# Attention pairs on one core: order of projections and pairs, banks of the turns, and the engine of some biases

## What is computed

```python
proj = h @ w_in[l]
qa, ka, va, qb, ckv, qi, ki, wi = jnp.split(proj, offsets, axis=-1)
out_a = dilated_mixture(qa, ka, va, slopes_a)      # A heads
q_lat = jnp.einsum('bthd,hdr->bthr', qb, w_uk[l])
o_lat = sparse_attention(qi, ki, wi * IDX_SCALE, q_lat, ckv, slopes_b)   # B heads
out_b = jnp.einsum('bthr,hrd->bthd', o_lat, w_uv[l])
x = x + ga1 * (jnp.concatenate([out_a, out_b]) @ w_out[l])
```

## Time and profile before

| | us |
|---|---|
| median of 3 runs | 2023.68 (2023.48 to 2025.96) |
| profiled execution | 2021.82, span 2020.0 |
| busy: PE, DVE, ACT, POOL | 1947.8, 1048.7, 447.2, 1183.6 |
| stretch of the eight pairs, 1515.80 to 1597.35 | 81.55, PE busy in 60.14 of it |

### The profile page before, as it was taken

The page is one execution under the profiler, slowest core; times in us unless marked ns, Lnnn a source line. Parts: engine busy times, 40 slices in busy tenths (PEclk is TensorE's granted clock), DMA queues, the critical chain, the costliest instruction groups (busy, mean ns, idle before and its releaser), DMA issues.

```text
span 2020.0 us, 25249 instructions
## 1 busy us (share of the span) xinstructions
PE 1947.8 (96%) x8772; PEld 1563.7 (77%) x8772; DVE 1048.7 (52%) x1588; ACT 447.2 (22%) x762; POOL 1183.6 (59%) x907
## 2 busy tenths in 40 slices
PE   7999999999999999998999999999997899999998
PEld 6787868888888877655888888886775588888886
DVE  5566257766646353557666663234857563232222
ACT  3302342112110022432221111012116421111100
POOL 3653325878877956223688787743550157666673
PEclk7999999999999999998999999999999999999999
DMA  7432223555555422111355553321210023232232
GB/s 298 167 125 73 94 94 104 188 187 203 188 200 179 156 91 83 42 42 46 133 201 193 194 188 127 104 95 63 84 63 22 11 84 104 93 101 97 95 113 73
DMA packets 67518, 242.25 MB, mean 120 GB/s; under 512 B 7642, under 2 KB 8026, under 8 KB 67458
## 3 DMA queue, kind: packets, MB, share of 16 engines
q1 hardware_dynamic: 65536, 237.01, 34.2%
q10 hardware_dynamic: 1922, 4.40, 0.6%
HBM read 239.28 MB, written 2.10 MB: 119 GB/s over the span
## 4 chain that ended last, share of the span: by engine, by line
PE 89%; DVE 4%; ACT 3%; issue 2%; DMA 1%; POOL 1%; SPq 0%; DVEq 0%; ACTq 0%; POOLq 0%
PE gemm L443 24%; PE gemm L445 23%; PE gemm L444 23%; PE gemm L470 2%; PE gemm L472 2%; PE gemm L471 2%; DMA w_raw<-wstream 1%; PE mix L646 1%; PE mix L443 1%; PE gemm L799 1%; PE mix L444 1%; PE mix L445 1%; PE mix L952 1%; PE gemm L813 1%; PE mix L554 1%
## 5 line engine op out<-in xcount | busy, mean ns | idle before, releaser
L427 POOL TENSOR_TENSOR w_lo<-w_raw,w_hi 128x1024 fp32r<-128x1024 f32 x302 | 741.1, 2454 | 25.2
L443 PE MATMUL gemm<-h_hi,w_hi 128*128 128x512 f32 x1616 | 635.4, 393 | 14.3 <-DVE h_lo L1123 6.4
L444 PE MATMUL gemm<-h_lo,w_hi 128*128 128x512 f32 x1616 | 631.1, 391 | 0.0
L445 PE MATMUL gemm<-h_hi,w_lo 128*128 128x512 f32 x1616 | 631.0, 390 | 0.0
L424 POOL TENSOR_TENSOR pool_gate<-pool_gate 128x1 f32<-128x1 f32 x298 | 104.2, 350 | 764.6 <-PE gemm L445 619.7
L443 PEld LDWEIGHTS gemm<-h_hi,w_hi 128*128 128x128 f32 x1616 | 305.0, 189 | 83.9 <-issue 13.4
L425 POOL TENSOR_SCALAR w_hi<-w_raw 128x1024 fp32r<-128x1024 f32 x302 | 351.1, 1163 | 18.4 <-DMA w_raw<-wstream 18.4
L445 PEld LDWEIGHTS gemm<-h_hi,w_lo 128*128 128x128 f32 x1616 | 304.7, 189 | 64.0
L444 PEld LDWEIGHTS gemm<-h_lo,w_hi 128*128 128x128 f32 x1616 | 305.2, 189 | 62.7
L1017 DVE CUSTOM_DVE_ANT_0 ada_raw<-ada_raw,c_act 128x1024 f32<-128x1024 f32 x128 | 219.4, 1730 | 106.2 <-DMA ada_raw<-adastream 106.2
L445 PE MATMUL gemm<-p_hi,w_lo 128*128 128x512 f32 x528 | 205.4, 389 | 0.0
(11 more groups left out here) (323 smaller groups left out, 1999.9 us busy)
## 6 DMA issues: line engine op xcount, KB each, us to landing
w_raw<-wstream SPq DMA_DIRECT2D x302, 512.0 KB, 3.5
ada_raw<-adastream SPq DMA_DIRECT2D x128, 512.0 KB, 4.3
a_early<-adastream SPq DMA_DIRECT2D x8, 1024.0 KB, 13.2
out<-x_res SPq DMA_DIRECT2D x8, 256.0 KB, 2.2
x_res<-x_in SPq DMA_DIRECT2D x2, 512.0 KB, 6.4
c_act<-c_in ACTq DMA_DIRECT2D x2, 512.0 KB, 7.2
x_res<-x_in ACTq DMA_DIRECT2D x2, 512.0 KB, 9.0
b_dist<-const_in ACTq DMA_DIRECT2D x1, 512.0 KB
```

The source lines that it names most:

```text
L427: pool.tensor_tensor(wlo[s][:], raw[:, u % RAW, :], whi[s][:].bitcast(F32), ALU.subtract).then_inc(w_split, 1)
L443: pe.matmul(out_ap, w_h, r_h, start=first, stop=False)
L444: pe.matmul(out_ap, w_h, r_l, start=False, stop=False)
L445: return pe.matmul(out_ap, w_l, r_h, start=False, stop=last)
```

## The change

The value chunks come first in `attn_in`, and their banks are evicted to `VA` right behind them. The A heads' query and key tiles alternate, so that the first four hold pairs 0 and 1. scores(0) start behind the latent values; then come the four tiles of pairs 2 and 3, scores(1), the first B query chunk, and the pairs. The other three B query chunks are cut into eighths and stand between the turns of pairs 0, 1 and 2 (`query_part`), in gemm bank 1; so the turns of pairs 0 to 3 use gemm bank 0 alone, each waiting for the copy of the one before. Since the high parts of the hidden state are still in use, ScalarE keeps the results of pairs 0 and 1 in T2 and makes their high parts at pair 2; VectorE makes the three low parts at p = 3. Biases of odd heads from head 5 on are made by GpSimd, in two instructions for an A head and five for a B head, between its splits of chunks (`bias` in its block); before each it waits for the logits four heads back. VectorE makes the even ones.

```diff
@@ -63,7 +63,7 @@
           ("ffn1", 44, (11, 11, 11, 11)), ("down1", 24, (2, 2, 2, 2)), ("idx_in", 6, (2, 2, 1, 1)),
-          ("attn_in", 16, (5, 5, 3, 3)), ("attn_out", 8, (2, 2, 2, 2)), ("ffn2", 44, (11, 11, 11, 11)),
+          ("attn_in", 16, (4, 7, 3, 2)), ("attn_out", 8, (2, 2, 2, 2)), ("ffn2", 44, (11, 11, 11, 11)),
@@ -430,11 +430,52 @@
                 split_at(u, 0, u, u >= SPL)
-            with pool.Fori(1, NCHUNK // 4) as b:
+            def one(n):
+                split_at(n, n // 4, n % 4, True)
+            steps = [0]
+            def bias(g):
+                if g == 5:
+                    pool.wait_ge(small_loaded, 112)
+                if g == 9:
+                    pool.wait_ge(sig("mask_rows"), 1)
+                pool.wait_ge(sig("att_z"), g - 3)
+                steps[0] += 1
+                if g < 8:
+                    pool.tensor_scalar(BI[:, g % 4, 0:T], DL[:, 0:T], -SLOPE_A[g], 0.0, ALU.mult, ALU.add).then_inc(sig("bias_slope"), 1)
+                    pool.wait_ge(sig("bias_slope"), steps[0])
+                    pool.tensor_tensor(BI[:, g % 4, 0:T], BI[:, g % 4, 0:T], DL[:, T:2 * T], ALU.add).then_inc(sig("att_b_odd"), 1)
+                else:
+                    pool.tensor_scalar(T2[:, 12, :], DL[:, 0:T], -SLOPE_B[g - 8], 0.0, ALU.mult, ALU.add).then_inc(sig("bias_slope"), 1)
+                    pool.wait_ge(sig("bias_slope"), steps[0])
+                    for j in range(NTB):
+                        seg = slice(OFF_J[j], OFF_J[j] + P * (j + 1))
+                        ins = pool.tensor_tensor(BI[:, g % 4, seg], T2[:, 12, 384 - P * j:T], SC[:, seg], ALU.add)
+                    ins.then_inc(sig("att_b_odd"), 1)
+                    pool.wait_ge(sig("att_b_odd"), steps[0])
+            ahead = N0["attn_out"] + 1
+            with pool.Fori(1, ahead // 4) as b:
                     split_at(4 * b + u, b, u, True)
-            for u in range(NCHUNK % 4):
-                split_at(NCHUNK // 4 * 4 + u, NCHUNK // 4, u, True)
+            for n in range(ahead // 4 * 4, ahead):
+                one(n)
+            for p in range(3):
+                bias(2 * p + 5)
+                one(ahead + p)
+            for g in range(11, 16, 2):
+                bias(g)
+            after = (ahead + 3 + 3) // 4
+            for n in range(ahead + 3, 4 * after):
+                one(n)
+            with pool.Fori(after, NCHUNK // 4) as b:
+                for u in range(4):
+                    split_at(4 * b + u, b, u, True)
+            for n in range(NCHUNK // 4 * 4, NCHUNK):
+                one(n)
@@ -917,15 +958,16 @@
             mm.then_inc(norm_sum, 1)
-            def attn_tiles(first):
-                for u in range(4):
-                    tile_chunk(N0["attn_in"] + first + u, (N0["attn_in"] + u) % SPL, u, G0["attn_in"][u] + first // 4)
-            attn_tiles(0)
+            def attn_tile(c, bank, use):
+                n = N0["attn_in"] + c
+                tile_chunk(n, n % SPL, bank, G0["attn_in"][bank] + use)
+            token_body(N0["attn_in"], N0["attn_in"], list(G0["attn_in"]))
             bcast(rstdps, bc[0])
-            attn_tiles(4)
+            for u in range(4):
+                attn_tile(4 + u, u, 1)
@@ -933,15 +975,14 @@
                 pe.matmul(M[j][:], T2[:, 5, j * P:(j + 1) * P], wuv[:], start=True, stop=True).then_inc(sig("vb_mm"), 1)
-            token_body(N0["attn_in"] + 8, N0["attn_in"] + 8, [g + 2 for g in G0["attn_in"]])
                 else:
-                    if p == 4:
-                        pe.wait_ge(gfree[1], G0["attn_out"][1])
+                    if p >= 4:
+                        pe.wait_ge(gfree[1], G0["attn_in"][1] + 3 + p - 3)
@@ -956,25 +997,45 @@
-            def turn(p, pieces):
-                for c in pieces:
-                    n = 5 * p + c
-                    pe.wait_ge(sig("att_p"), 2 * p + (1 if c < 2 else 2))
-                    if n < 2:
-                        pe.wait_ge(gfree[n], G0["attn_out"][n])
-                    else:
-                        pe.wait_ge(sig("att_c"), n - 1)
-                    for a, i, o in PIECES[c]:
-                        z = Z[(2 * p + a) % 4]
-                        for j in range(i, NTB):
-                            mm = pe.transpose(G[n % 2][:, o + P * (j - i):o + P * (j - i) + P],
-                                              z[:, OFF_J[j] + i * P:OFF_J[j] + (i + 1) * P], const("ident"))
-                    mm.then_inc(sig("att_t"), 1)
+            def turn_bank(n):
+                return G[0] if n < 20 else G[n % 2]
+            def turn(p, c):
+                n = 5 * p + c
+                pe.wait_ge(sig("att_p"), 2 * p + (1 if c < 2 else 2))
+                if n == 0:
+                    pe.wait_ge(gfree[0], G0["attn_out"][0])
+                elif n <= 20:
+                    pe.wait_ge(sig("att_c"), n)
+                else:
+                    pe.wait_ge(sig("att_c"), n - 1)
+                for a, i, o in PIECES[c]:
+                    z = Z[(2 * p + a) % 4]
+                    for j in range(i, NTB):
+                        mm = pe.transpose(turn_bank(n)[:, o + P * (j - i):o + P * (j - i) + P],
+                                          z[:, OFF_J[j] + i * P:OFF_J[j] + (i + 1) * P], const("ident"))
+                mm.then_inc(sig("att_t"), 1)
+            def query_part(u, first, count):
+                n = N0["attn_in"] + 12 + u
+                s = n % SPL
+                if first == 0:
+                    pe.wait_ge(w_split, n + 1)
+                    pe.wait_ge(gfree[1], G0["attn_in"][1] + 3 + u)
+                for k in range(first, first + count):
+                    mm = three(G[1][:], whi[s][:, k * P:(k + 1) * P], wlo[s][:, k * P:(k + 1) * P],
+                               Hhi[:, k, :], Hlo[:, k, :], k == 0, k == KT - 1)
+                if first + count == KT:
+                    mm.then_inc(pe_done, 1)
                     pe.wait_ge(gfree[2], G0["attn_out"][2])
+                elif p < 3:
+                    pe.wait_ge(sig("att_kept"), p)
@@ -988,16 +1049,29 @@
             scores(0)
-            for u in range(2):
-                tile_chunk(N0["attn_in"] + 12 + u, (N0["attn_in"] + u) % SPL, u, G0["attn_in"][u] + 3)
+            for u, (bank, use) in enumerate(((0, 2), (1, 2), (2, 2), (0, 3))):
+                attn_tile(8 + u, bank, use)
             scores(1)
-            for u in range(2):
-                tile_chunk(N0["attn_in"] + 14 + u, (N0["attn_in"] + 2 + u) % SPL, u, G0["attn_in"][u] + 4)
+            query_part(0, 0, KT)
             for p in range(8):
-                turn(p, (0, 1))
+                parts = p < 3
+                turn(p, 0)
+                if parts:
+                    query_part(p + 1, 0, 2)
+                turn(p, 1)
+                if parts:
+                    query_part(p + 1, 2, 2)
                     scores(p + 2)
-                turn(p, (2, 3, 4))
+                turn(p, 2)
+                if parts:
+                    query_part(p + 1, 4, 2)
+                turn(p, 3)
+                if parts:
+                    query_part(p + 1, 6, 1)
+                turn(p, 4)
+                if parts:
+                    query_part(p + 1, 7, 1)
@@ -1559,7 +1633,7 @@
                 ins = dve.tensor_scalar(SC[:, seg(j)], SC[:, seg(j)], 0.5 * TAKEN, NEG, ALU.is_gt, ALU.mult)
-            link(ins)
+            ins.then_inc(sig("mask_rows"), 1)
@@ -1575,7 +1649,10 @@
                 dve.wait_ge(sig(f"att_s{g % 2}"), g // 2 + 1)
-                dve.wait_ge(sig("att_b"), g + 1)
+                if g % 2 and g >= 5:
+                    dve.wait_ge(sig("att_b_odd"), g // 2 - 1)
+                else:
+                    dve.wait_ge(sig("att_b"), g + 1 if g < 4 else g // 2 + 3)
@@ -1597,7 +1674,8 @@
                 dve.wait_ge(hhi_ready, KT * 7 + k + 1)
-                dve.tensor_tensor(Hlo[:, k, :], G[2][:], Hhi[:, k, :].bitcast(F32), ALU.subtract).then_inc(h_ready, 1)
+                src = T2[:, 10 + k, :] if k < 2 else G[2][:]
+                dve.tensor_tensor(Hlo[:, k, :], src, Hhi[:, k, :].bitcast(F32), ALU.subtract).then_inc(h_ready, 1)
@@ -1610,8 +1688,10 @@
                     bias(2 * p + 4)
-                    bias(2 * p + 5)
-                if p >= 1:
+                if p == 3:
+                    pair_low(0)
+                    pair_low(1)
+                if p >= 3:
@@ -1973,19 +2053,23 @@
-            for u in range(4):
-                evict(u, u, 10 + u, 0.125)
-            for u in range(4):
-                evict(4 + u, u, 14 + u)
+            act.wait_ge(pe_done, N0["attn_in"] + 4)
+            for j in range(4):
+                act.activation(VA[:, j, :], G[j][:], ACT.Copy).then_inc(gfree[j], 1)
+            evict(4, 0, 10, 0.125)
+            evict(5, 1, 14)
+            evict(6, 2, 11, 0.125)
+            evict(7, 3, 15)
                 act.activation(VB[:, j, :], M[j][:], ACT.Copy).then_inc(sig("vb_copied"), 1)
-            act.wait_ge(pe_done, N0["attn_in"] + 12)
```

(27 more changed lines are left out.)

## The result

The changed kernel takes **2030.36 us** (median of 9 runs, 2028.61 to 2033.22) against 2023.48 (9 runs beside them, 2021.89 to 2026.18): a ratio of **1.0035, 95% interval 1.0026 to 1.0045**, so slower by 6.9 us. The forecast was 2026.7, slower by 3.0; its range (2019 to 2032) holds the result, the narrower band of the forecast itself (2024.5 to 2029.5) doesn't. In the profiled executions the span grew from 2020.0 to 2027.0 us.

A forecast was written before the change was run, and what follows sets the result against it. Head pairs bound by a ring through ScalarE's exponentials and copies and VectorE's logits, not by TensorE; -1.0 (start and rings) + 0.6 (collisions) + 3.4 (clock) = +3.0 us, so 2026.7 us, range 2019 to 2032.

The forecast's parts named there:

- the ring: Cycle of one head pair through exponentials, scores and turns: 10.6 us before the change, 16.0 with a query chunk added.
- the starved rival: GpSimd keeps the port through split and bias, so VectorE's normalising waits; up to 8.8 us, 2029 to 2033; chance 0.20.
- Start: Beginning of the attention stage: scores of pair 0 start at 1464.0, scores of pair 1 end at 1490.7.
- The wait before the second turn of pair 0: TensorE waits 2.5 us for ScalarE's first copy, queued behind head 2's exponentials; second turn starts at 1501.0.
- The ring of pairs 0 to 2: 15.2 us a pair against 16.0, with a 1.9 us wait for the copy; filling gains 0.8 us a pair.
- T: Start of a pair's fifth turn on TensorE; predicted 1508.7 for pair 0 and 1553.4 for pair 3.
- Pair 2 to 3: Two kept high parts add 0.98 us on ScalarE; wait of 4.2 us, then 14.3 us between the fifth turns.
- GpSimd: Its splits and biases hold VectorE's normalising, mostly hidden by the wait for the copy; +0.6 us in all.
- Clock: TensorE falls to half clock behind the waits of 2.5 and 4.2 us, 1.7 us each: +3.4 us.
- The sum at full clock: Fifth turn of pair 3 at 1553.4 against 1554.44, so -1.0 us before collisions and clock falls.
- The filled rival: ScalarE reaches its first copy earlier, so waits of 2.5, 1.9, 1.9 and 1.6 us vanish: 2015.4 us; chance 0.12.
- The full-clock rival: No clock falls behind the new waits: -0.4, 2023.3 us, or 2021 if the late fall goes too; chance 0.25.

The follow-up runs named there:

- split moved: Changed kernel, but GpSimd's first late split (first attn_out chunk) waits for the negated maximum of head 3; 2028.64 us, 1.0035 of the kernel before.
- copy early: Changed kernel, but in pairs 0 to 3 ScalarE copies the first turned piece before the even head's exponentials; 2027.03 us, 1.0022 of the kernel before.
- GpSimd quiet: Changed kernel, but all biases on VectorE and each of four late splits waiting until the next pair's even head is normalised; 2027.15 us, 1.0019.
- both: Changed kernel with the first turned piece copied before the exponentials, all biases on VectorE and the four late splits delayed; 2017.45 us, 0.9975.
- filled waits: Changed kernel with twelve idle matmuls of 256 columns before the second turns of pairs 0 and 3; 2027.68 us, 1.0024 of the kernel before.
- two banks in pair 3: Run with both edits, plus two banks for pair 3's turns and the fourth late split waiting until all heads are normalised; 2015.81 us, 0.9962.

## Why the prediction was right, and where it was short

The direction, the place and the ring's mechanism were right; the size was short by 3.9 us. Two things in this are luck. The direction rested on the clock: without it the forecast was -0.4, and without the clock's 5.9 us the change measured about +1.1. And 2030.36 lies above the forecast's own band (2024.5 to 2029.5), where the range reached only for the starved rival, which didn't come about in the change. By its steps:

- **Start.** First scores 1464.0 predicted, 1463.87 measured. The new start by itself, which the sum has as waits and a half-clock stretch saved, is bounded by the run that has only it: 188.12 to 184.62 us, of which 1.5 is the half clock of before in the second pair.
- **The wait before the second turn of pair 0: 2.5 predicted, 4.36 measured.** This is the step that failed. I took the logits as never held, which they aren't, and let head 2's exponentials start behind them at 1498.1. I left out the small instruction behind the logits that negates the maximum. It reads and writes SBUF alone, the split held it for 2.33 us, and the second turn began at 1503.29 instead of 1501.0: **+2.3 us** (PE was free 0.5 us later than I said, so the wait itself grew by 1.9). With the split moved the wait was 2.21 us. All sixteen of these instructions took 0.17 us in the kernel before, so its own rows gave no sign; but the normalising held for 3.99 us in the earlier trace rows is the same kind of instruction, and the step didn't carry that over.
- **The ring of pairs 0 to 2.** T to T 15.2 predicted, 15.11 and 15.09 measured; waits 1.9 predicted, 1.67 and 1.66 measured. The reason given (the query work stands inside the ring and the copy behind the exponentials) is half of it: the copy early alone left T to T at 15.05, GpSimd quiet alone at 15.08, and only both brought 13.23 us. VectorE's chain was as long as ScalarE's, as the step's own figures had it (scores possible by T + 9.4, wanted at 9.43). That the query chunks gain less than the wait they stand in for is right.
- **Pair 2 to 3.** A wait of 4.2 predicted, 4.09 measured; 14.3 at full clock predicted, 15.90 measured, of which the scores at half clock are 1.6 (1552.82 to 1556.86, 4.04 us, against 2.46). What the two kept high parts add to this wait was not tested by itself.
- **GpSimd.** +0.6 predicted for its collisions, 0.1 measured behind T of pair 0: the biases on VectorE gave no gain, GpSimd quiet gave 0.1 us behind T of pair 0, and the normalising, held to 3.2 us, was hidden by the wait for the copy, as the step says. The cost of GpSimd's stream stood elsewhere, in the split at the start. The step was also right about what happens without that cover: a milder form of the starved rival appears in the run with the copy early, with waits of 1.74 and 1.83 us for logits, less than the 2.9 to 3.2 of its price.
- **Clock.** Two falls of 1.7 us were predicted behind the two long waits; both came, the first costing 2.7 us and the second 1.6 (both shown by the filled waits). A third, of 1.6 us, came behind the wait of 1.94 in pair 4 (scores 4.04 us), of a kind that the sum had counted as none; no run was made to test it.

The sum at full clock was -1.0; with rings 0.2 shorter it is -1.2. To this come 2.3 (held maximum), 2.7, 1.6 and 1.6 (clock): +7.0, against 6.9 measured. Against the forecast of +3.0 that is 2.3 for the one held instruction, 2.5 for the clock (5.9 instead of 3.4), and -0.8 for the two small terms taken too high (0.6 of collisions, 0.2 of the ring).

The filled rival (2015.4) didn't come about for the reason that the prediction gave against it, the order in the code; with that order changed and GpSimd quiet its time is nearly reached (2017.45, 2015.81). The full-clock rival failed on three falls.

## What to carry to other kernels

When filler work is put into a waiting engine's ring, ask first whether what ends the wait (here a copy queued behind two groups of exponentials on ScalarE) moves forward too; if it doesn't, the ring grows by the filler and gains little. Two chains of nearly equal length hide each other's cost: in the ring of pairs 0 to 2 neither edit alone shortened T to T (15.05 and 15.08 us against 15.11), both together gave 13.23, so a single edit that gives little is no proof that its cause is small. Where one engine's instructions can hold another's, put them where the other has nothing on the path, and look at the small instructions on the path too, not only at the busiest.

## What the runs showed of the hardware that was not expected

**A four-column instruction held for a whole GpSimd instruction.** VectorE's negated maximum (128x4) took 0.17 us alone, and 2.33 and 2.36 us (the change, copy early) behind a GpSimd split instruction of 2.36 and 2.38 us that had just started. The logits (one input from PSUM, one from SBUF) aren't held: beside the split instruction of 1479.54 to 1482.26 in the change the largest took 0.68 us (1480.95), and the negated maximum right behind it (1481.67, 0.61 us) ended only with the split. The Trainium skill ("SBUF — State Buffer", section "Who interferes with whom") says that `tensor_scalar` can take the port pair that VectorE shares with GpSimd, that whoever issues first keeps it for the whole instruction, and that an instruction with at most one SBUF input outside those modes doesn't contend; both rows agree. The prediction had used this rule for the big instructions only.

**The clock doesn't follow the length of the wait alone.** The scores ran at half clock, or fell to it, behind waits of 1.94 us (the change), 1.83 (copy early) and 2.21 with two eighths between (first split moved), and at full clock behind 1.94 (biases on VectorE), 2.48 (filled waits) and 2.64 (two banks in pair 3). In the change's own trace the scores behind one wait of 1.94 us ran at half clock (1566.45, 1.97 us) and behind the next wait of 1.94 at full clock (1578.67, 1.31 us). What decides it in a given execution was not settled. A wait of about 2 us on the path can cost nothing or 1.6 us (scores 4.04 instead of 2.46), and the sum should have carried both ends.
